# Expert gate and up weights read as one 16 KB stretch per partition, with the gathered rows turned by every fourth column

## The chip, the cores and the metric

The kernel runs on one core of a Trainium2 chip. The metric is device time in microseconds (us) of one execution. All weights and activations are float32; TensorE works on them either as float32 or, where a value has been split into a high and a low part, as rounded float32.

## The reference

The program is two transformer blocks; the change concerns the first, which has two layers (`DEPTH = 2`). In each layer 512 tokens of 1,024 values go through a modulated norm, attention and a convolution, and then through sixteen experts that each pick their own 64 tokens:

```python
def expert_choice_ffn(h, w_router, w_gate, w_up, w_down):
    cap = CAPACITY_FACTOR * S // N_EXPERTS                     # 64
    aff = jax.nn.softmax(jnp.einsum('bsd,de->bse', h, w_router), axis=-1)
    gate, idx = lax.top_k(aff.transpose(0, 2, 1), cap)
    xe = jax.vmap(lambda hb, ib: hb[ib])(h, idx)               # gathered rows
    hid = jax.nn.silu(jnp.einsum('becd,edf->becf', xe, w_gate)) * jnp.einsum('becd,edf->becf', xe, w_up)
    ye = jnp.einsum('becf,efd->becd', hid, w_down) * gate[..., None].astype(h.dtype)
    ...                                                        # scattered back and added
# in the layer: h2 = rms_norm(x, norm2_g[l]) * (1.0 + scale2) + shift2
```

`w_gate`, `w_up` and `w_down` are each 1,024 by 1,024 for each expert and layer, 4 MB in float32, so the experts of one layer need 192 MB.

## The kernel before

One pass of the loop over the layers is a block in which each engine has its own instruction stream, and all waits are semaphore waits written by hand. SyncE (SP) issues nearly all transfers, in program order, on one queue.

**The experts' weights.** Each of the three matrices of an expert is read in two halves, so an expert `e` has six chunks of 2 MB, `j` = 0, 1 (gate), 2, 3 (up), 4, 5 (down). A chunk lies as 128 partitions by 4 by 1,024 values, 16 KB in each partition. `load(e, j)` issues one. For down, partition p takes four neighbouring rows of the matrix, which lie in memory as one run of 16 KB (`(h p k)`); for gate and up it takes rows p, p + 128, p + 256, p + 384 of the half, four runs of 4 KB (`(h k p)`). There are six places in the tile `ring` and two early ones; a chunk is loaded into a place as soon as TensorE has used the chunk that stood there (`chunk_used`). Eight chunks (six of expert 0, gate of expert 1) are read before the experts begin; each of the other 88 follows a use.

**The tokens.** Experts are worked in pairs `n`. `gather(n)` picks 128 token rows out of `h_high3` and `h_low3`, which hold x / rms(x), and puts them in PSUM; ScalarE copies them to `x_rows` [128 rows, 1,024]. `turn_tokens(n)` turns them in 8 pieces of 128 columns, so that the width stands on the partitions; VectorE multiplies by `smod` (norm gain times 1 + scale2) and adds `mod` (shift2), which both hold one value for each (partition, kt), and writes `x_e`. `expert` then multiplies: for each chunk j and each k of 4, two products of 64 stationary columns with 512 moving values. The sum over the width runs over partition and k, so rows of weights and pieces of tokens have to be cut in the same way. `hidT` is already turned by every fourth column (`hid_apart`) to fit the down weights.

**The place of the small products.** In the attention part, TensorE (from line 663 on) makes tiles of values (L663), then the router's bias (`mod` times `w_r`, L684, into PSUM bank 3), then waits for VectorE's `kd` (L1211) and spreads the first head's key factors (L679). VectorE multiplies the first head's keys by them (L1217, L1218), and the scores and the softmax (L711, L1233, L993) follow. VectorE copies the router's bias out of bank 3 in the first step of the softmax loop (L1252).

Of the kernel before, what the change touches and what calls it, by code (L numbers as in the profile page):

```python
# [12 lines left out]
P = 128  # L13
D = 1024
KT = D // P
S = 512
TT = S // P
# [9 lines left out]
EXPERTS, CAP = 16, 64  # L27
# [20 lines left out]
SHIFT1, SCALE1, GATE1, SHIFT2, SCALE2, GATE2 = (m * KT for m in range(N_MOD))  # L48
# [3 lines left out]
GROUP = 32  # L52
# [235 lines left out]
def layer(nc, A, sem, M, l, ahead):  # L288

    ps, const, xT, ring, scr = M["ps"], M["const"], M["xT"], M["ring"], M["scr"]
    ident, rot = const[:, C_IDENT:C_IDENT + P], const[:, C_ROT:C_ROT + P]
# [10 lines left out]
    vec, convw, mod, smod = (M[n] for n in ("vec", "convw", "mod", "smod"))  # L303
# [41 lines left out]
    GATHER_BANKS = (0, 5)  # L345
# [15 lines left out]
    rbias = M["rbias"]  # L361
    rankm, gcol = M["krg_r"][0:EXPERTS, :], M["gcol"]
    sel_pair = M["hy_r"][0:EXPERTS, 7 * S - P:7 * S]
    x_e, sg, hid = (scr[:, 0, :], hy[:, 7 * S:8 * S]), scr[:, 1, :], scr[:, 2, :]
    x_rows = hy[:, D:2 * D]
    hidT, hid_apart = sg, hid.rearrange("p (n b) -> p b n", b=4)
    s_pair = M["scr_r"][:, 3, :].rearrange("p (t n) -> p t n", t=TT)
    h_high3 = M["one_hot_T_r"][:, 0:CHUNK].rearrange("p (t d) -> p t d", t=TT)
# [3 lines left out]
    c_spread, ada_used, ada_rows, ada_cols, mod_ready = (sem(n) for n in ("c_spread", "ada_used", "ada_rows", "ada_cols", "mod_ready"))  # L372
# [16 lines left out]
    r_bias_mm, r_bias_kept, r_scaled, xe_scaled, sel_built = (sem(n) for n in ("r_bias_mm", "r_bias_kept", "r_scaled", "xe_scaled", "sel_built"))  # L389
# [21 lines left out]
    with nc.Block() as block:  # L411
        @block.sync
        def _(sp):
            w_ada = at("w_ada").rearrange("a (k p) n -> p (a k) n", p=P)
            w = at("w_in").rearrange("a (k p) n -> p (a k) n", p=P)

            def ada_chunk(c):
                before = max(b for b in range(c) if ADA_PLACES[b] == ADA_PLACES[c])
                sp.wait_ge(ada_used, before + 1)
                sp.dma_start(ada[c], w_ada[:, :, HALF * c:HALF * (c + 1)]).then_inc(ada_in[ADA_PLACES[c]], 16)  # L420

            load_input(sp, A, M, l, w_in_in)
            ada_chunk(4)
            for piece, then in ((2, (5,)), (CT, (6,)), (3, range(7, 12))):
                if piece < CT:
                    for i in (2 * piece, 2 * piece + 1):
                        sp.dma_start(w_in[i], w[:, :, in_cols[i]:in_cols[i] + P]).then_inc(w_in_in[piece], 16)
                else:
                    sp.wait_ge(ahead["tables"], 16)
                    sp.dma_start(ring[:, CHUNK:CHUNK + KT * first].rearrange("p (k n) -> p k n", k=KT), w[:, :, 0:first]).then_inc(w_in_in[piece], 16)  # L430
                for c in then:
                    ada_chunk(c)
            sp.wait_ge(ada_used, 12)
            sp.dma_start(w_uq, at("w_uq").rearrange("a (k p) n -> p (a k) n", p=P)).then_inc(uq_in, 16)
            sp.dma_start(w_ukv, at("w_ukv").rearrange("a p n -> p (a n)")).then_inc(uq_in, 16)
            sp.dma_start(ring[:, TABLES:TABLES + 2 * S], A["rope"]).then_inc(uq_in, 16)
            sp.dma_start(w_r[:, :, 0:EXPERTS], at("w_router").rearrange("a (k p) n -> p (a k) n", p=P)).then_inc(w_r_in, 16)
            w = at("w_out").rearrange("a (k p) n -> p (a k) n", p=P)
            for k in range(0, KT, 4):
                sp.dma_start(w_out[:, k:k + 4], w[:, k:k + 4]).then_inc(w_out_in, 16)  # L440

            def load(e, j):
                name, half = ("w_gate", "w_up", "w_down")[j // 2], j % 2
                w = A[name][bass.ds(l, 1), bass.ds(e, 1)]
                if name == "w_down":
                    w = w.rearrange("a e (h p k) n -> h p (a e k) n", h=2, k=4)
                else:
                    w = w.rearrange("a e (h k p) n -> h p (a e k) n", h=2, k=4)
                place, landed, _ = expert_chunk(e, j)
                sp.dma_start(place, w[half]).then_inc(landed, 16)  # L450

            sp.wait_ge(pv_done, HEADS)
            for j in (1, 2, 3):
                load(0, j)
            sp.wait_ge(cmix, CT)
            load(1, 1)
            sp.wait_ge(wout_done, KT)
            for e, j in ((0, 0), (0, 4), (0, 5), (1, 0)):
                load(e, j)
            for n in range(6):  # L460
                sp.wait_ge(chunk_used, n + 1)
                load(1 + (n + EARLY) // 6, (n + EARLY) % 6)

            with sp.If(l < DEPTH - 1):
                load_rows(sp, A, M, (l + 1) % DEPTH, ahead)
            with sp.If(l > DEPTH - 2):
                sp.wait_ge(chunk_used, 8)
                sp.dma_start(mem_tok, A["mem_2"][0].rearrange("(t p) d -> p t d", p=P)).then_inc(mem_in, 16)
                for i, name in enumerate(("ln_mem_g_2", "ln_mem_b_2")):
                    sp.dma_start(rowsA[KT * i:KT * (i + 1), :], A[name].rearrange("(k p) -> k p", p=P)).then_inc(mem_in, 16)  # L470

            def shifted(e, j):
                sp.wait_ge(chunk_used, 6 * e + (j - 5))
                load(e, j)

            for j in range(EARLY, 6):
                shifted(2, j)
            with sp.Fori(3, EXPERTS) as e:
                for j in range(6):
                    shifted(e, j)  # L480
            with sp.If(l < DEPTH - 1):
                after, used = (l + 1) % DEPTH, 6 * EXPERTS
                for c in range(3):
                    sp.wait_ge(chunk_used, used - (5 - c))
                    load_ada(sp, A, M, after, c, ahead)
                sp.wait_ge(xe_mm, 2 * PAIRS)
                load_ada(sp, A, M, after, 3, ahead)
            with sp.If(l > DEPTH - 2):
                sp.wait_ge(st_mm, PAIRS)
                load_mixer(sp, A, M, ahead)  # L490
# [23 lines left out]
        def _(pe):  # L514
# [49 lines left out]
            for at_tile, i in enumerate(IN_ORDER):  # L564
                bank = at_tile % 6
                if at_tile == 0:
                    pe.wait_ge(w_in_ready, 2)
                    for kt in range(KT):
                        pe.wait_ge(h_low_ready, kt + 1)
                        for n in range(2):  # L570
                            pe.matmul(ps[:, n, :], w_in_high[n][:, kt, :], h_high[:, kt, :], start=(kt == 0), stop=False)
                            pe.matmul(ps[:, n, :], w_in_high[n][:, kt, :], h_low[:, kt, :], start=False, stop=False)
                            mm = pe.matmul(ps[:, n, :], w_in_low[n][:, kt, :], h_high[:, kt, :], start=False, stop=(kt == KT - 1))
# [41 lines left out]
            for i in range(10):  # L615
# [6 lines left out]
                out = ps[:, i % 6, :]  # L622
# [57 lines left out]

            pe.wait_ge(w_r_in, 16)
            pe.wait_ge(pad_zero, 1)
            for kt in range(KT):
                mm = pe.matmul(ps[:, 3, 0:GROUP], mod[:, SHIFT2 + kt:SHIFT2 + kt + 1].to_broadcast([P, P]), w_r[:, kt, :], start=(kt == 0), stop=(kt == KT - 1))  # L684
            mm.then_inc(r_bias_mm, 1)
# [117 lines left out]
            def turn_tokens(n):  # L803
                for half in range(2):
                    pe.wait_ge(xe_kept, 2 * n + (half + 1))
                    for b in range(4):
                        kt = 4 * half + b
                        mm = pe.transpose(ps[:, GATHER_BANKS[half], b * P:(b + 1) * P], x_rows[:, kt * P:(kt + 1) * P], ident)
                    mm.then_inc(xeT_mm, 1)

            def gates(n):
# [288 lines left out]
        def _(dve):  # L1100
# [129 lines left out]
            for i in range(4 * HEADS + 1):  # L1230
# [18 lines left out]
                        next(conv)  # L1249
                if i == 0:  # L1250
                    dve.wait_ge(r_bias_mm, 1)
                    dve.tensor_copy(rbias[:], ps[:, 3, 0:EXPERTS]).then_inc(r_bias_kept, 1)  # L1252
                if 7 <= i < 7 + KT:
                    kt = i - 7
                    dve.wait_ge(w_out_split, kt + 1)
# [60 lines left out]
            def build(n, ranks):  # L1316
                dve.tensor_tensor(s_pair.rearrange("p t (r s) -> p t r s", r=2), slot_row.rearrange("p (r s) -> p r s", r=2).unsqueeze(1).to_broadcast([P, TT, 2, CAP]),
                                  ranks[:, :, bass.ds(2 * n, 2)].unsqueeze(3).to_broadcast([P, TT, 2, CAP]), ALU.is_equal).then_inc(s_built, 1)
                for r in range(2):
# [3 lines left out]
            x_parts = [x.rearrange("p (b n) -> p b n", b=4) for x in x_e]  # L1323
            x_turned = [ps[:, bank, :].rearrange("p (b n) -> p b n", b=4) for bank in GATHER_BANKS]
            x_scale, x_shift = ([x[:, 4 * half:4 * half + 4].unsqueeze(2).to_broadcast([P, 4, P]) for half in range(2)]
                                for x in (smod[:, KT:2 * KT], mod[:, SHIFT2:SHIFT2 + KT]))

            def tokens(n):
                for half in range(2):
# [73 lines left out]
def memory1(nc, ctx, M):  # L1403
    M = dict(M)
    shared = dict(hy=[P, 2 * KT * S], h_tok=[P, TT * D], one_hot_T=[P, EXPERTS * S], ring=[P, 6 * TT * D])
    with ExitStack() as rounded:
        halves = dict(ring=[P, 3 * TT * D], ring2=[P, 3 * TT * D], scr=[P, 4, S], krg=[P, S])
        for name, shape in {**shared, **halves}.items():
            M[name + "_r"] = rounded.enter_context(nc.sbuf_tensor(name + "_r", shape, FR))
    for name, shape in dict(  # L1410
        **shared, scr=[P, 4, S],
        krg=[P, S], c_col=[P, KT], vec=[P, NVEC], convw=[P, TAPS * CT],
        mod=[P, N_MOD * KT], smod=[P, 2 * KT], stat=[P, 112],
        lg=[P, TT, EXPERTS], aff=[P, TT, EXPERTS], rankT=[P, TT, EXPERTS], top8=[EXPERTS, 8],
        gcol=[P, 2], rbias=[P, EXPERTS],
    ).items():
        M[name] = ctx.enter_context(nc.sbuf_tensor(name, shape, F32))
    return M
# [1537 lines left out]
```

## Time and profile before

| | |
|---|---|
| time, median of 3 runs | 2585.97 us (2582.03 to 2588.11) |
| the profiled execution | span 2585.9 us; no other time is given for it |
| TensorE busy | 2354.7 us, 91% of the span |
| VectorE, ScalarE, GpSimd busy | 43%, 35%, 10% |
| the DMA queue of SP | 637.98 MB, 64.9% of 16 engines' span |
| mean granted TensorE clock | 0.975 |

Busy shares are averages over stages that have different limits. The expert stages of the two layers lie at about 320 to 787 us and 1095 to 1557 us; they have to be read by themselves. A "releaser" in a row is what ended the idle time of an engine.

### The profile page before, as it was taken

How to read it: one execution, taken by the hardware profiler on the slowest of the kernel's cores; microseconds unless marked ns; L12 is line 12 of the kernel's file. 1: busy time of each engine (PE TensorE's matmuls, PEld its weight loads, DVE VectorE, ACT ScalarE, POOL GpSimd, SP SyncE). 2: the span in 40 equal slices, each digit the busy share in tenths (PEclk: the TensorE clock that was granted, in tenths of full speed). 3: DMA queues.
4: the chain of work that ended last, by engine and by line, in shares of the span. 5: the costliest groups of instructions: out<-in, count | busy, mean ns of one | idle time of the engine just before them, and what ended most of it. 6: DMA issues, size and time to landing. Idle time of an engine off the chain costs nothing. (4 is left out here: it accounts for less than half of the span.)

```text
span 2585.9 us, 31066 instructions
## 1 busy us (share of the span) xinstructions
PE 2354.7 (91%) x12565; PEld 1481.8 (57%) x12565; DVE 1124.8 (43%) x1686; ACT 913.2 (35%) x1228; POOL 268.8 (10%) x245
## 2 busy tenths in 40 slices
PE   6999799888886999799888888999999999989997
PEld 5735534333335835544333337887888777767776
DVE  4985312111214985412111225647521112459897
ACT  4256211111114256211111116656632234247775
POOL 0000100000000000100000005000254433300000
PEclk8999899999998989899999999999999999989999
DMA  9702499999999602499999995522223421159995
GB/s 343 286 1 93 168 381 415 415 416 417 417 413 345 220 1 96 164 399 415 415 417 417 416 411 170 169 82 82 82 76 100 134 66 59 56 184 378 365 366 212
DMA packets 252020, 650.48 MB, mean 252 GB/s; under 512 B 12144, under 2 KB 110718, under 8 KB 243454
## 3 DMA queue, kind: packets, MB, share of 16 engines
q1 hardware_dynamic: 248180, 637.98, 64.9%
q0 software_dynamic: 2592, 7.87, 0.8%
q10 hardware_dynamic: 1130, 2.99, 0.3%
q8 instruction: 83, 1.36, 0.2%
q14 instruction: 35, 0.29, 0.0%
HBM read 641.99 MB, written 8.39 MB: 252 GB/s over the span
## 5 line engine op out<-in xcount | busy, mean ns | idle before, releaser
L841 PE MATMUL ps<-ring,hy 128*64 128x512 f32 x992 | 225.1, 596 | 46.5 <-DMA ring<-in_w_up 31.8
L841 PE MATMUL ps<-ring,scr 128*64 128x512 f32 x992 | 225.1, 596 | 30.3 <-DMA ring<-in_w_up 28.1
L1347 DVE TENSOR_TENSOR scr<-scr,ps 128x512 f32<-128x512 f32 x32 | 22.0, 687 | 528.9 <-PE ps L841 528.9
L1614 POOL TENSOR_TENSOR raw_r<-raw,w_high 128x512 fp32r<-128x512 f32 (+1 forms) x160 | 189.8, 1219 | 435.0 <-ACT w_high L1882 435.0
L868 PE MATMUL ps<-ring,scr 128*64 128x512 f32 x1024 | 227.2, 596 | 3.1 <-ACT scr L1058 2.7
L1637 PE MATMUL ps<-x_high,w_high 128*128 128x512 f32 x464 | 186.4, 402 | 5.7 <-DVE y L2278 5.7
L1639 PE MATMUL ps<-x_high,raw_r 128*128 128x512 f32 x464 | 184.2, 397 | 0.0
L1638 PE MATMUL ps<-xT_r,w_high 128*128 128x512 f32 x464 | 183.1, 395 | 0.0
L2703 DVE TENSOR_TENSOR ring_r<-ring,ring_high 128x2048 fp32r<-128x2048 f32 x77 | 172.7, 2283 | 22.3 <-ACT ring_high L2626 22.3
L841 PEld LDWEIGHTS ps<-ring,hy 128*64 128x64 f32 x992 | 68.5, 137 | 198.2 <-issue 122.0
L841 PEld LDWEIGHTS ps<-ring,scr 128*64 128x64 f32 x992 | 68.2, 137 | 180.2 <-issue 122.2
L1135 DVE SCALAR_TENSOR_TENSOR one_hot_T<-h_tok,convw,one_hot_T 128x512 f32<-128x512 f32 x240 | 166.3, 745 | 1.8
L868 PEld LDWEIGHTS ps<-ring,scr 128*64 128x64 f32 x1024 | 70.5, 137 | 139.9 <-issue 129.1
L2626 ACT ACTIVATE ring_high<-ring 128x2048 fp32r<-128x2048 f32 x77 | 144.1, 1916 | 17.9 <-DMA ring<-in_w_up 16.4
L1882 ACT ACTIVATE w_high<-raw 128x2048 fp32r<-128x2048 f32 (+1 forms) x58 | 105.9, 1826 | 95.9 <-DMA raw<-in_p_b 48.9
L1067 ACT ACTIVATE hy<-ps,gcol 64x512 f32<-64x512 f32 x64 | 43.7, 682 | 255.7 <-PE ps L868 255.3
L1637 PEld LDWEIGHTS ps<-x_high,w_high 128*128 128x128 f32 x464 | 87.6, 189 | 27.6 <-DVE y L2278 6.2
L1638 PEld LDWEIGHTS ps<-xT_r,w_high 128*128 128x128 f32 x464 | 87.5, 189 | 22.8 <-issue 2.2
L1639 PEld LDWEIGHTS ps<-x_high,raw_r 128*128 128x128 f32 x464 | 87.4, 188 | 19.0
L2561 PE MATMUL ps<-ring_high,xg_high 128*128 128x512 f32 x224 | 92.7, 414 | 0.0
L1058 ACT ACTIVATE scr<-ps 128x512 f32<-128x512 f32 x32 | 19.1, 596 | 203.4 <-PE ps L853 203.4
L1049 ACT ACTIVATE hy<-ps 128x512 f32<-128x512 f32 x32 | 19.1, 598 | 194.3 <-PE ps L800 194.3
(589 smaller groups left out, 4582.2 us busy)
## 6 DMA issues: line engine op xcount, KB each, us to landing
ring<-in_w_up SPq DMA_DIRECT2D x64, 2048.0 KB, 23.8
ring<-in_w_down SPq DMA_DIRECT2D x64, 2048.0 KB, 22.3
ring<-in_w_gate SPq DMA_DIRECT2D x60, 2048.0 KB, 24.5
ring<-in_w_up SPq DMA_DIRECT2D x56, 1024.0 KB, 7.3
ring<-in_w_ada SPq DMA_DIRECT2D x22, 2048.0 KB, 13.3
ring<-in_w_down SPq DMA_DIRECT2D x28, 1024.0 KB, 7.4
raw<-in_w_in SPq DMA_DIRECT2D x24, 1024.0 KB, 5.1
raw<-in_w_in SPq DMA_DIRECT2D x20, 512.0 KB, 5.2
```

Source lines behind the costliest of these rows:

```text
L841: mm = pe.matmul(ps[CAP * half:CAP * (half + 1), 1 + j // 2, :], x_e[j % 2][:, at_x:at_x + CAP], weights[:, k, half * HALF:(half + 1) * HA ...
L868: mm = pe.matmul(ps[CAP * half:CAP * (half + 1), 4, :], hidT[:, at_f:at_f + CAP], weights[:, k, half * HALF:(half + 1) * HALF], start=(j = ...
L1067: made = act.activation(out[:, half * HALF:(half + 1) * HALF], ps[rows, 4, :], ACT.Identity, scale=gcol[rows, r:r + 1])
L1135: op = dve.scalar_tensor_tensor(acc[:, c, :], src, w, acc[:, c, :], ALU.mult, ALU.add)
L1614: part = pool.tensor_tensor(dst[:, a:a + 2], src[:, a:a + 2], high[:, a:a + 2].bitcast(F32), ALU.subtract)
L1637: pe.matmul(out, s_high, m_high, start=(n == 0), stop=False)
L1638: pe.matmul(out, s_high, m_low, start=False, stop=False)
L1639: mm = pe.matmul(out, s_low, m_high, start=False, stop=(n == len(terms) - 1))
L1882: act.activation(slot_of(w_high, n), landed_chunk(n), ACT.Copy).then_inc(w_split, 1)
L2561: pe.matmul(ps[:, n % 2, :], xh[i % 2][:, kt, :], h[:, k, :], start=(kt == 0), stop=False)
L2626: act.activation(high[q], raw[q], ACT.Copy).then_inc(w_split, 1)
L2703: dve.tensor_tensor(low[q], raw[q], high[q].bitcast(F32), ALU.subtract).then_inc(w_ready, 1)
```

## The change

Gate and up weights are read as down weights are: partition p takes rows 4p to 4p + 3 of a half. To fit, the gathered rows are turned by every fourth column of a half, and the two modulation vectors are put in the same order once in each layer: 32 small products with every fourth column of the identity (two vectors, four groups g, four k) write a [128, 16] piece into PSUM bank 3 beside the router's bias, and VectorE copies it into the new tile `xmod`, from which the expert part takes scale and shift.

```diff
+    x_apart = x_rows.rearrange("p (h n b) -> p h b n", h=2, b=4)
+    xmod = M["xmod"]
+    every_fourth = ident.rearrange("p (r k) -> p k r", k=4)
...
-                if name == "w_down":
-                    w = w.rearrange("a e (h p k) n -> h p (a e k) n", h=2, k=4)
-                else:
-                    w = w.rearrange("a e (h k p) n -> h p (a e k) n", h=2, k=4)
+                w = w.rearrange("a e (h p k) n -> h p (a e k) n", h=2, k=4)
...
             pe.wait_ge(pad_zero, 1)
+            pe.wait_ge(mod_ready, 3)
+            for n, vector in enumerate((smod[:, KT:2 * KT], mod[:, SHIFT2:SHIFT2 + KT])):
+                halves = vector.rearrange("p (h g) -> p g h", h=2)
+                for g in range(TT):
+                    out = ps[GROUP * g:GROUP * (g + 1), 3, GROUP + KT * n:GROUP + KT * (n + 1)].rearrange("p (h k) -> p k h", h=2)
+                    for k in range(4):
+                        pe.matmul(out[:, k, :], every_fourth[:, k, :], halves[:, g, :], start=True, stop=True)
...
-                        kt = 4 * half + b
-                        mm = pe.transpose(ps[:, GATHER_BANKS[half], b * P:(b + 1) * P], x_rows[:, kt * P:(kt + 1) * P], ident)
+                        mm = pe.transpose(ps[:, GATHER_BANKS[half], b * P:(b + 1) * P], x_apart[:, half, b, :], ident)
...
-                    dve.tensor_copy(rbias[:], ps[:, 3, 0:EXPERTS]).then_inc(r_bias_kept, 1)
+                    step(dve.tensor_copy(rbias[:], ps[:, 3, 0:EXPERTS]))
+                    dve.tensor_copy(xmod[:], ps[:, 3, GROUP:GROUP + 2 * KT]).then_inc(r_bias_kept, 1)
...
-                                for x in (smod[:, KT:2 * KT], mod[:, SHIFT2:SHIFT2 + KT]))
+                                for x in (xmod[:, 0:KT], xmod[:, KT:2 * KT]))
```

TensorE's stream in the attention part, before (each row is a group of products; `hy` holds `kd` in the row L679):

```order
L670 MATMUL ps<-const,hy 128x128 x4
L663 MATMUL ps<-ring,h_tok 128x512 x2
L684 MATMUL ps<-h_tok,mod 128x32 x8
L679 MATMUL ps<-hy,ones 128x512
L663 MATMUL ps<-ring,h_tok 128x512
```

And of the changed kernel, whose lines are numbered 7 higher from there on:

```order
L670 MATMUL ps<-const,hy 128x128 x4
L663 MATMUL ps<-ring,h_tok 128x512 x2
L689 MATMUL ps<-smod,const 32x2 x16
L689 MATMUL ps<-mod,const 32x2 x16
L691 MATMUL ps<-h_tok,mod 128x32 x8
L679 MATMUL ps<-hy,ones 128x512
L663 MATMUL ps<-ring,h_tok 128x512
```

Thirty-two calls of 32 by 2 stand ahead of the router's bias, and so ahead of the first head's key factors. Nothing else in TensorE's stream moves.

SP's stream where the first experts' chunks are issued, before:

```order
L450 DMA ring<-in_w_up 128x4x1024 x2
L450 ISA
L450 DMA one_hot_T<-in_w_gate 128x4x1024
L450 DMA ring<-in_w_gate 128x4x1024
L450 DMA ring<-in_w_down 128x4096 x2
```

And changed:

```order
L450 DMA ring<-in_w_up 128x4096 x2
L450 ISA
L450 DMA one_hot_T<-in_w_gate 128x4096
L450 DMA ring<-in_w_gate 128x4096
L450 DMA ring<-in_w_down 128x4096 x2
```

The order of the transfers stays; the gate and up rows now have the shape that down has, one run for each partition instead of four.

## Rows read from the trace of the kernel before

**Rows 1.** Busy time by stretch, whole expert stages and pieces of the first one.
```profile
core 0: us, PE busy (x) PEld busy (x) DVE busy (x) ACT busy (x) POOL busy (x), PEclk, DMA share, GB/s
320.40:787.00 466.60, 422.26 (x1967) 172.21 (x1971) 99.00 (x178) 60.40 (x92) 0.00 (x0) 1.00 1.01 407
336.00:436.00 100.00, 99.31 (x475) 41.48 (x476) 19.58 (x37) 14.52 (x22) 0.00 (x0) 1.00 1.00 404
436.00:536.00 100.00, 90.22 (x424) 38.80 (x422) 22.17 (x37) 11.51 (x18) 0.00 (x0) 1.00 1.02 415
636.00:736.00 100.00, 87.72 (x412) 35.97 (x410) 18.66 (x34) 12.56 (x19) 0.00 (x0) 1.00 1.02 416
```

**Rows 2.** TensorE's waits in each expert stage: total us, times, longest.
```profile
PE ps L841 <- DMA ring<-in_w_up: 29.9, 22, 1.5
PE ps L841 <- DMA ring<-in_w_gate: 7.4, 5, 1.5
...
PE ps L841 <- DMA ring<-in_w_up: 30.0, 22, 1.5
PE ps L841 <- DMA ring<-in_w_gate: 7.3, 5, 1.5
```

**Rows 3.** TensorE in time order: first wait for weights, a free-running expert, last chunk.
```profile
389.12 7.09 PE L868 MATMUL ps<-ring,scr 128*64 128x512 f32 x32
416.44 7.09 PE L868 MATMUL ps<-ring,scr 128*64 128x512 f32 x32
456.95 3.65 PE L841 MATMUL ps<-ring,scr 128*64 128x512 f32 x16 [1.44 <-DMA ring<-in_w_up]
774.67 3.65 PE L868 MATMUL ps<-ring,scr 128*64 128x512 f32 x16 [0.17 <-DMA ring<-in_w_down]
```

**Rows 4.** Packets of three stretches: 836 to 850, 1191 to 1204, 1207 to 1214 us.
```profile
DMA packets 2667, 5.42 MB, mean 387 GB/s; under 512 B 33, under 2 KB 33, under 8 KB 2664
DMA packets 1334, 5.32 MB, mean 410 GB/s; under 512 B 34, under 2 KB 34, under 8 KB 1334
DMA packets 202, 3.05 MB, mean 435 GB/s; under 512 B 16, under 2 KB 16, under 8 KB 16
```

**Rows 5.** Busy time by stretch: one kind of transfer in each.
```profile
835.00:850.00 15.00, 15.00 (x178) 12.26 (x177) 11.03 (x15) 3.05 (x5) 0.00 (x0) 1.00 1.04 387
1191.00:1204.00 13.00, 13.00 (x66) 4.56 (x64) 5.49 (x11) 2.42 (x3) 0.00 (x0) 1.00 1.03 410
1207.00:1214.00 7.00, 7.00 (x34) 3.03 (x31) 1.64 (x3) 0.00 (x0) 0.00 (x0) 1.00 1.02 435
1237.50:1244.00 6.50, 6.50 (x29) 3.46 (x30) 0.69 (x1) 0.60 (x1) 0.00 (x0) 1.00 0.99 423
```

**Rows 6.** All engines in time order around the router's bias, layer 0.
```profile
159.96 1.87 PE L684 MATMUL ps<-h_tok,mod 128*128 128x32 f32 x16
162.60 1.13 PE L679 MATMUL ps<-hy,ones 128*128 128x512 f32 x2 [0.77 <-DVE hy L1211]
165.27 1.12 PE L711 MATMUL ps<-ring 128*128 128x512 f32 x2 [0.69 <-ACT ring L986]
171.00 0.17 DVE L1252 COPY rbias<-ps 128x16 f32<-128x16 f32 x1
```

**Rows 7.** Small products: a run of 32 by 128, and L684's single durations.
```profile
213.68 1.08 PE L517 MATMUL ps<-scr,ones 128*32 128x128 f32 x32
...
L684 PE MATMUL ps<-h_tok,mod x32: 193/276/277, 160.0 to 932.0; 128*128 128x32 f32 x32
```

**Rows 8.** Groups of the turns, strided (L853) and not (L808), 400 to 750 us.
```profile
L853 PE MATMUL ps<-const,scr 128*128 128x128 f32 x48 | 7.6, 280 | 0.0
L808 PE MATMUL ps<-const,hy 128*128 128x128 f32 x48 | 6.6, 280 | 0.0
```

**Rows 9.** Busy time by stretch: the same 155 us of the two layers.
```profile
155.00:310.00 155.00, 129.51 (x626) 74.49 (x616) 86.58 (x166) 77.44 (x135) 9.85 (x8) 0.96 0.27 108
926.00:1081.00 155.00, 134.48 (x614) 75.44 (x610) 82.81 (x159) 77.29 (x134) 9.85 (x8) 0.92 0.25 98
```

More of the change, by code:

```diff
@@ L1414, in memory1 @@
         lg=[P, TT, EXPERTS], aff=[P, TT, EXPERTS], rankT=[P, TT, EXPERTS], top8=[EXPERTS, 8],
-        gcol=[P, 2], rbias=[P, EXPERTS],
+        gcol=[P, 2], rbias=[P, EXPERTS], xmod=[P, 2 * KT],
     ).items():
```

## The prediction

> **What bounds the kernel now.** I read the busy time by stretch first. In the expert stage of the first layer the DMA engines are busy for a share of 1.01 and TensorE for 422 of 467 us [rows 1]. The pieces of that stage differ: from 336 to 436 us TensorE is busy 99.31 of 100 us and the transfers run at 404 GB/s; from 436 us on TensorE has 10 to 12 us of idle time in each 100, and the transfers stand at 415 to 416 GB/s. The second view, TensorE's waits, says what ends that idle time: in each layer 37.3 us are waits for gate and up chunks (29.9 + 7.4, and 30.0 + 7.3) [rows 2]. In time order the first such wait comes at 456.95 us, and the last down chunk is still waited for at 774.67 us [rows 3]. So for the first five experts TensorE lives on the eight chunks read ahead, and then the DMA queue sets the pace. One expert that waits for nothing takes TensorE 416.44 - 389.12 = 27.3 us [rows 3] (every second one has less beside it and takes less), while its 12.58 MB at 415.5 GB/s take 30.3 us.
>
> The third view is the DMA traffic of stretches that hold one kind of transfer. From 1191 to 1204 us there are 1,300 larger packets in 5.32 MB, 4 KB each: gate and up. From 1207 to 1214 us there are 186 of 16 KB: down. From 836 to 850 us, modulation weights come in packets of 2 KB [rows 4]. With the engines always busy, the three move at 387 (2 KB), 410 (4 KB) and 435 or 423 GB/s (16 KB, two stretches) [rows 5]. A window of 7 us over packets of 16 KB is coarse, so I work out their rate from the long windows: one expert is 30.28 us at 415.5 GB/s [rows 1], its four chunks of 4 KB packets take 4 x 2.097 MB / 410 = 20.46 us, so its two down chunks take 9.82 us, 4.91 us each, or 427 GB/s. A gate or up chunk takes 5.115 us.
>
> **The change part by part.**
>
> *The transfers.* A gate or up chunk becomes what a down chunk is now, in shape, size and destination. I price it at 4.91 us: 0.205 us less. Of a layer's 64 gate and up chunks, six are read ahead while TensorE does other things (four of expert 0, two of expert 1), at no gain; 58 follow a use. If the queue never ran dry that would be 58 x 0.205 = 11.9 us per layer. It does run dry at first: the 404 GB/s of 336 to 436 us against 415.5 [rows 1] is 2.8 us in which transfers waited for TensorE to free a place. There a faster transfer only waits sooner. That stretch serves 3.3 experts, 0.82 us each, so up to 2.7 us of the gain may be lost there; as most of the idle time there lies in few gaps, I take 0.9. That leaves 11.0 us per layer (9.2 to 11.9), 22.0 us for both. It fits under the waits that it shortens, 37.3 us per layer, and an expert would still take the queue 29.5 us against 27.3 of TensorE, so the queue stays the bound. What comes behind the stage hangs on its end: the last down chunk (its wait is at 774.67 us), then the scatter and the next layer. SP's next transfers wait for the same uses and come forward with them. So I count the gain in full.
>
> The rate has two ends: with 435 GB/s a chunk takes 4.82 us and the gain is 58 x 0.295 - 0.9 = 16.2 us per layer; with 423 GB/s it takes 4.96 us and the gain is 58 x 0.157 - 0.9 = 8.2. I stay at 427, which comes from 300 us and not from 7.
>
> The Trainium skill speaks against this term: DMA: Bandwidth & Descriptors, Specifications, gives 512 B as the least transfer for line rate, by which 4 KB pieces are already at full rate and longer ones bring nothing. By that rule this trace should show equal rates; it shows 410 for 4 KB and 427 for 16 KB, and disagrees.
>
> *The added products.* 32 calls, each two instructions as everywhere in float32 (8 calls of L684 are 16 instructions [rows 6]), so 64 per layer. None of this shape is in the trace. L517 has the same 32 stationary columns and a wider moving side: 32 instructions in 1.08 us, 34 ns each [rows 7]. But its neighbours go to four different groups of columns in turn, the added ones four times in a row to the same group. L684, with 128 stationary columns, is the other end: 16 in 1.87 us, 117 ns each [rows 6]. From below 64 x 34 ns = 2.2 us, from above 7.5 us. They are nearest to L517; I take 45 ns, 2.9 us.
>
> Where they stand, that is nearly all on the path. TensorE ends L684 at 161.83 us and waits 0.77 us for `kd`, which comes at 162.54 [rows 6]; this slack hides the first 0.77 us. The rest, 2.1 us, delays the key factors (L679), behind them the fourth tile of values, ScalarE's copy of it, and the scores, which wait for that copy already now (0.69 us, at 165.27 us). Behind the scores stand the softmax of all heads, w_out and the router. Only when w_out is done does SP issue the last chunks ahead, and the experts start from the router, so nothing takes the delay back.
>
> *VectorE's copy.* One more copy of 128 by 16: 0.17 us [rows 6], between taps and the second maximum. I put 0.1 us of it on the path (0 to 0.2). The new wait for `mod_ready` was passed before, at the broadcast of the latent norms, and costs nothing.
>
> *The turns.* They read `x_rows` with a step of four. The turn of `hid` does that now (L853): 280 ns on average, as L808 without a step: 280 ns [rows 8]. Nothing. `xmod` instead of `smod` and `mod` changes no size.
>
> Sum per layer: -11.0 + 2.1 + 0.1 = -8.8 us; two layers -17.6. The profiled span is 2585.9 us, the median 2585.97 us, so both serve: 2568.3 us.
>
> **The rivals.**
>
> 1. *The added products run at the spacing of L684.* 7.5 - 0.77 + 0.1 = 6.8 us per layer: 2585.9 - 22.0 + 13.6 = 2577.5. For it: four neighbours in one group of columns. Against it: a quarter of the columns to load.
>
> 2. *The granted clock.* The same 155 us of the two layers have 0.96 and 0.92 of full speed, and TensorE is busy 129.51 and 134.48 us in them, although they do the same work [rows 9]: about 5 us hang on where the clock falls to the lower of its two levels, 1.2 GHz. The change moves and slightly alters TensorE's activity right at the start of this stretch. One such fall more or less: 2573.3 or 2563.3. Nothing in the rows says which.
>
> 3. *The transfers gain nothing.* If gate and up reads are slow for where they lie and not for their packets, the queue stays at 415.5 GB/s, and only the added work remains: 2585.9 + 4.4 = 2590.3, 0.17% slower. Against it: the three rates rise with packet size, and all three are reads of the same kind of tensor.
>
> 4. *The other side: the added products don't overlap at all.* One alone takes 276 ns (L684) [rows 7]; the 117 ns are its spacing. If each waits for the end of its neighbour, because both go to the same group and bank, 64 x 0.276 = 17.7 us stand ahead of the key factors, 17.0 per layer on the path: 2585.9 - 22.0 + 34.0 = 2597.9, slower by 0.5%. It decides from (11.0 + 0.77) / 64 = 184 ns each. Against it: L684's neighbours go to one place too, all into the same sum, and overlap.
>
> **How the numbers follow.** The likeliest case (transfers at 427 GB/s, products at 34 to 60 ns) has 0.66, rival 1 has 0.10, rival 2 has 0.07 for each sign, rival 3 has 0.06, rival 4 has 0.04. The predicted time is that of the first, 2568.3 us. Its own range, from the queue's loss at the start (9.2 to 11.9), the products (2.2 to 3.8 us) and half of the way to the two rates, is 2562 to 2574. Over all, the low side reaches to 2558 (435 GB/s gives 2557.9), the high side to 2578, past rival 1. What a measurement of this kernel can tell from no change is about 0.2%, 5 us. Faster by more than that: all but rivals 3 and 4, 0.90. Rival 3 lies within 0.2%: 0.06. Slower: 0.04.
>
> **What the profile of the changed kernel would show.** The packets of the expert stages are 16 KB for all six chunks and the rate in each 100 us is 427 GB/s; at 418 or less the first term is more than three quarters off. TensorE's waits for gate and up are about 26 us per layer. Each expert stage is about 11 us shorter. The added products take 2.2 to 3.8 us in each layer, the wait of L679 for `kd` is gone, and from their start to the start of the expert stage the time is 2.2 us longer, at the same clock. The prediction is wrong if the rate stays at 415, if the products take over 7 us, or if TensorE's waits vanish and the stage doesn't get shorter, which would mean that TensorE is the bound before I think so.

## The result, and the profile after

The changed kernel takes 2570.18 us (median of 4 runs, 2564.83 to 2573.45), the kernel before 2587.01 us beside it. The ratio of the runs is 0.9946, with a 95% interval of 0.9932 to 0.9960: 14 us, or 0.54%, faster (the two medians by themselves lie 16.8 us apart). The profiled execution has a span of 2571.7 us, 14.2 us less than before. Of all executions used below one is left out, of the kernel `products_only`, which took 6070 us.

The busy time by stretch, the same 100 us windows and the same columns as before [rows 1]:

```profile
336.00:436.00 100.00, 98.45 (x470) 41.46 (x468) 18.86 (x35) 13.93 (x21) 0.00 (x0) 1.00 0.98 410
436.00:536.00 100.00, 94.39 (x444) 40.56 (x441) 20.88 (x37) 12.10 (x19) 0.00 (x0) 1.00 1.01 428
636.00:736.00 100.00, 91.02 (x425) 37.58 (x422) 19.23 (x35) 12.56 (x19) 0.00 (x0) 1.00 1.01 429
```

The queue runs at 428 to 429 GB/s where it ran at 415 to 416, and TensorE's idle time there is smaller. The packets of a stretch that held gate and up chunks before (1191 to 1204 us) are now 16 KB (338 larger packets in 5.54 MB), and the waits of TensorE in the first and in the second expert stage are shorter and come later, the first at 467.40 us (456.95 before [rows 3]):

```profile
DMA packets 375, 5.54 MB, mean 426 GB/s; under 512 B 37, under 2 KB 37, under 8 KB 37
```
```profile
PE ps L847 <- DMA ring<-in_w_up: 20.3, 21, 1.2
PE ps L847 <- DMA ring<-in_w_gate: 5.5, 5, 1.1
...
PE ps L847 <- DMA ring<-in_w_up: 20.6, 21, 1.3
PE ps L847 <- DMA ring<-in_w_gate: 5.5, 5, 1.1
```
```profile
467.40 3.65 PE L847 MATMUL ps<-ring,hy 128*64 128x512 f32 x16 [0.58 <-DMA ring<-in_w_up]
```

TensorE around the router's bias in layer 0, in order of time (before: [rows 6]; L691 is the router's bias, L718 the first scores):

```profile
159.51 1.26 PE L689 MATMUL ps<-smod,const 128*32 128x2 f32 x29
160.78 1.24 PE L689 MATMUL ps<-mod,const 128*32 128x2 f32 x29
161.95 2.75 PE L691 MATMUL ps<-h_tok,mod 128*128 128x32 f32 x16
164.51 2.05 PE L679 MATMUL ps<-hy,ones 128*128 128x512 f32 x2
168.96 2.08 PE L718 MATMUL ps<-ring 128*128 128x512 f32 x2 [0.69 <-ACT ring L992]
```

The added products take 161.95 - 159.51 = 2.44 us, 38 ns per instruction, and L679 waits for nothing any more. But the router's bias takes 2.75 us where it took 1.87, L679 takes 2.05 us where it took 1.13, and the first scores come 3.7 us later than before: behind the products the granted clock is at the lower level in this execution. Three windows show it, one of the kernel before and two of the changed one:

```profile
163.50:180.00 16.50, 13.48 (x33) 4.32 (x31) 13.43 (x27) 7.55 (x15) 0.00 (x0) 1.00 0.00 0
```
```profile
163.50:180.00 16.50, 15.81 (x22) 5.33 (x21) 7.82 (x16) 4.43 (x8) 0.00 (x0) 0.50 0.00 0
155.00:310.00 155.00, 138.64 (x678) 78.77 (x674) 79.72 (x154) 76.87 (x133) 7.68 (x7) 0.92 0.22 89
```

Cutting both executions at three places in each layer (the start of the turns L670, the start of the first expert's first product, the end of the last down product), from the starts of those rows, gives where the 14.2 us are:

| stretch, us | before | after | difference |
|---|---|---|---|
| start to L670 of layer 0 | 157.81 | 157.26 | -0.6 |
| L670 to the experts, layer 0 | 162.63 | 170.73 | +8.1 |
| experts, layer 0 | 457.88 | 446.52 | -11.4 |
| to L670 of layer 1 | 149.89 | 150.69 | +0.8 |
| L670 to the experts, layer 1 | 167.27 | 170.76 | +3.5 |
| experts, layer 1 | 458.22 | 446.78 | -11.4 |
| second block | 1032.20 | 1028.96 | -3.2 |

So the transfers give 22.8 us, the two stretches with the added products take back 11.6 us, and the rest is spread. How much of the 11.6 us belongs to the products and how much to this one execution, a second profile of the same kernel tells (`after_again`, another execution):

```profile
161.74 1.97 PE L691 MATMUL ps<-h_tok,mod 128*128 128x32 f32 x16
166.19 1.12 PE L718 MATMUL ps<-ring 128*128 128x512 f32 x2 [0.69 <-ACT ring L992]
```
```profile
163.50:180.00 16.50, 14.35 (x36) 4.82 (x35) 12.55 (x27) 6.54 (x13) 0.00 (x0) 1.00 0.00 0
```

Here the clock is at full speed behind the same products. From L670 (at 157.05 us) to the first scores it is 9.14 us, against 7.46 us in the kernel before and 11.70 us in the first profile. So at full clock the products cost 1.7 us on the path, and the 2.6 us beside them in the first profile went with the clock.

### The profile page after: what moved, and what is told of

It is laid out like the page before. It is cut to its first block and busy times, and to the rows that moved or that the text cites. A ratio compares the mean times of both kernels' runs of the same rounds, so it can differ in the third digit from the quotient of the medians.

```text
span 2571.7 us, 31324 instructions
## 1 busy us (share of the span) xinstructions
PE 2371.3 (92%) x12693; PEld 1495.2 (58%) x12693; DVE 1126.1 (44%) x1688; ACT 912.9 (35%) x1228; POOL 268.7 (10%) x245
## 5 line engine op out<-in xcount | busy, mean ns | idle before, releaser
L847 PE MATMUL ps<-ring,hy 128*64 128x512 f32 x992 | 225.0, 595 | 37.1 <-DMA ring<-in_w_up 26.1
L847 PE MATMUL ps<-ring,scr 128*64 128x512 f32 x992 | 224.5, 594 | 16.8 <-DMA ring<-in_w_up 14.7
L2570 PE MATMUL ps<-ring_high,xg_low 128*128 128x512 f32 x224 | 87.7, 392 | 0.0
```

The costliest lines, as they stand in the source:

```text
L847: mm = pe.matmul(ps[CAP * half:CAP * (half + 1), 1 + j // 2, :], x_e[j % 2][:, at_x:at_x + CAP], weights[:, k, half * HALF:(half + 1) * HA ...
L2570: mm = pe.matmul(ps[:, n % 2, :], xl[i % 2][:, kt, :], h[:, k, :], start=False, stop=(kt == KT - 1))
```

## The experiments

All ratios are of a kernel's runs to runs of the kernel before on the same chip.

### The parts alone: `transfers_only`, `products_only`

```diff
 transfers_only: the changed kernel, and
-            pe.wait_ge(mod_ready, 3)
-            for n, vector in enumerate(...):  ... 32 products
-                    dve.tensor_copy(xmod[:], ps[:, 3, GROUP:GROUP + 2 * KT])...
-                                for x in (xmod[:, 0:KT], xmod[:, KT:2 * KT]))
+                                for x in (smod[:, KT:2 * KT], mod[:, SHIFT2:SHIFT2 + KT]))
 products_only: the kernel before, with the 32 products and the copy
```

> The changed kernel without the 32 added products and the second copy; scale and shift are taken from smod and mod in their old order, so the tokens are modulated wrongly. Theory 1 (the transfers give the gain, and the added products cost more than their own 2.4 us per layer, because the granted clock falls right behind them): both expert stages stay 11.4 us shorter than before, the stretches ahead of them are as before, so 2587.0 - 22.8 = 2564.2 us, ratio 0.9912, and the fall of the clock at 163 us of layer 0 is gone. Rival (the clock fell there by chance of its phase): the products' own 1.7 us per layer are saved, 2570.2 - 3.4 = 2566.8 us, and the clock may fall anywhere.

> The kernel before with the 32 added products and the second copy in each layer, and nothing else; what they make is not used. Theory 1: the clock falls behind them in both layers, as it does in the changed kernel, so +8.0 and +3.4 us as its trace has them: 2598.4 us, ratio 1.0044. Rival: only what they take beyond the wait that they fill, 1.8 us per layer: 2590.6 us, ratio 1.0014, with the clock at full speed behind them in layer 0.

`transfers_only`: 2562.8 us, ratio 0.9920 (0.9901 to 0.9938). Its expert stages are 447.63 and 447.60 us. The ratio doesn't decide: theory 1 gives 0.9912 and the rival 0.9922, and both lie in the interval. The stages are 10.3 and 10.6 us shorter than before, of the 11.4 that were expected. But the clock did fall in its layer 0 (its stretch from L670 is 167.04 us, as long as that of layer 1 before, and its clock from 155 to 310 us is 0.93), so a fall there needs no products. That part of theory 1 is refuted as it was put.

`products_only`: 2590.37 us, ratio 1.0028 (1.0015 to 1.0040). By the ratio it is 7.2 us more (3.9 to 10.3), between the two theories' 3.6 and 11.4, and the interval holds neither. Its expert stages are 458.06 and 458.15 us, as before. Where its clock hardly fell (layer 0), the stretch from L670 is 165.35 us, 2.7 more than in the kernel before; in layer 1 it is 170.58 us, 3.3 more.

### The products elsewhere, and more of them: `products_late`, `products_x4`, `late_x4`

```diff
 products_late: the changed kernel, the products moved behind turn_rows, ahead of the wait for the ranks
+                    out = ps[GROUP * g:GROUP * (g + 1), 7, 2 * P + KT * n:2 * P + KT * (n + 1)].rearrange("p (h k) -> p k h", h=2)
             pe.wait_ge(rank_ready, 1)
...
             step(dve.tensor_copy(rankT[:], turned))
+            step(dve.tensor_copy(xmod[:], ps[:, 7, 2 * P:2 * P + 2 * KT]))
 products_x4 (at the change's place), late_x4 (at the late place):
-            for n, vector in enumerate((...)):
+            for n, vector in 4 * tuple(enumerate((...))):
```

> The changed kernel with the 32 products put where TensorE waits 10.5 us for the ranks (L796 in the changed kernel), into bank 7, and copied there. Both theories: the products cost nothing there. Theory 1: no fall of the clock at 163 us either, so as without the products: 2564.2 us, 0.9976 of the changed kernel, ratio to before 0.9912. Rival: 2566.8 us. If the products in the new place lie on the path after all, 2 to 3 us per layer more.

> The changed kernel with the 32 products made four times over in each layer (the same values written again). They take 2.44 us once in the trace, so 7.3 us more per layer: 2570.2 + 14.6 = 2584.8 us by both theories, ratio to before 0.9992. If it is the sparse work of these products that makes the clock fall (theory 1), four times as much makes it fall earlier, partly within them, and for longer: another 2 to 5 us per layer, up to 2594 us. By the rival nothing beyond the 14.6 us.

> The changed kernel with the products in TensorE's wait for the ranks, as before, but made four times over there. Their work of 4 x 2.6 us just fills the 10.5 us of the wait. Theory 1 (it is the place that costs, not the products): no time more than with the products late once, ratio 0.9915, within 1 us per layer, and the clock at 0.974. Rival (products of this kind lower the clock wherever they stand): mean clock 0.969 as with four times in front, and 3 to 6 us more.

`products_late`: 2560.0 us, ratio 0.9915 (0.9899 to 0.9931). It has the lowest time of the kernels that leave nothing out. TensorE makes the products where it waited 10.47 us for the ranks, and still waits:

```profile
298.28 1.26 PE L792 MATMUL ps<-smod,const 128*32 128x2 f32 x29
308.63 0.60 PE L795 MATMUL ps<-const,krg_r 16*128 16x16 f32 x4 [7.84 <-DVE krg_r L1317]
```

The stretches from L670 to the experts are 162.52 and 164.11 us, the lowest of all profiles; in `late_again`, the same kernel, they are 165.64 and 167.25 us. There the ratio is 0.9911 (0.9892 to 0.9930). The ratios of both theories, 0.9912 and 0.9922, lie in both intervals; from 163.5 to 180 us the clock is at full speed in both profiles, as theory 1 had it, but that is so in `after_again` too.

> The kernel with the products late, beside the kernel before on one more chip. Ratio 0.9915 (0.990 to 0.993), mean clock 0.974, expert stages of 447 us, rank stretch of both layers 1.9 us plus the clock's share shorter than in the changed kernel.

`products_x4`: 2583.34 us, ratio 1.0000 (0.9989 to 1.0011), so 14 us more than the changed kernel's 0.9946 has, and 16 more than the 0.9937 of its second measurement; 14.6 were expected by the rival. Of the 2 to 5 us per layer that theory 1 put on top, the upper part is refuted: 2594 us would be a ratio of 1.0027, above the interval. In its trace the four rounds take 8.84 us in each layer, 6.4 more than one round's 2.44, so 12.8 of the 14 to 16 us are the rounds themselves, and little is left for the clock (part of its lower level lies over the added products there, which don't notice it, as the last section shows). `late_x4`: 2561.65 us, ratio 0.9918 (0.9898 to 0.9937), as late once. The three more rounds, 192 instructions in each layer, cost about 15 us at the one place and nothing that can be told at the other: it is the place. The clock speaks for that too: `late_x4` has a mean of 0.973, the 0.974 of theory 1 and not the rival's 0.969.

### The packets: `runs_8k`, `runs_2k`, `down_4k`

The tokens of these three are turned as in the changed kernel, so their expert outputs are other ones; the work of the engines and the bytes are the same. In `runs_8k` and `runs_2k` the place in the ring is cut in the same way as the weights.

```diff
 runs_8k, gate and up:
+                    w = w.rearrange("a e (h k p q) n -> h p (a e k) (q n)", h=2, k=2, q=2)
 runs_2k, gate and up:
+                    w = w.rearrange("a e r (c n) -> a e (r c) n", c=2).rearrange("a e (h k p) n -> h p (a e k) n", h=2, k=8)
 down_4k, down only:
+                    w = w.rearrange("a e (h k p) n -> h p (a e k) n", h=2, k=4)
```

> The changed kernel with gate and up read in two runs of 8 KB per partition (weights and tokens no longer fit together, so the output of the experts is another). Theory 1 (each packet costs a fixed 8.4 ns beside its bytes: 4 KB at 410 GB/s is 159.8 ns per engine, 16 KB at 427 is 613.9, so 0.0370 ns per byte and 8.4 ns): 8 KB take 311 ns, 421 GB/s, a chunk 4.98 us, and each expert stage is 58 x 0.07 = 4 us longer than the 446.7 of the changed kernel: 451 us; 2578 us in all. Rival (what counts is that a partition's rows lie in one piece, not the length of the packets): the 458 us of before; 2593 us.

> The changed kernel with gate and up read in eight runs of 2 KB per partition (again another output). Theory 1: 2 KB take 75.7 + 8.4 = 84.1 ns, 390 GB/s, a chunk 5.38 us, 58 x 0.47 = 27 us more per stage than 446.7: 474 us; 2625 us in all. Rival (a partition's rows in one piece or not): as with 4 KB, 458 us and 2593 us. A second rival (runs shorter than the 4 KB of before are no worse, since the engines fill a packet from several): also 458 us.

> The changed kernel with the down weights read as gate and up were before, in four runs of 4 KB per partition (another output), so the two kinds have changed places. Theory 1: 30 down chunks of a layer behind the start take 0.205 us more each, 6.2 us: stages of 453 us and 2582.5 us in all. Rival (it was gate and up, whose chunks TensorE waits for, and down chunks are never late, so their length costs nothing): stages of 447 us, 2570 us.

| kernel | gate, up / down packets | expert stages, us | expected | ratio |
|---|---|---|---|---|
| `runs_2k` | 2 / 16 KB | 474.0, 475.5 | 474 | 1.0148 (1.0133 to 1.0162) |
| before | 4 / 16 KB | 457.9, 458.2 | | 1 |
| `down_4k` | 16 / 4 KB | 453.2, 454.1 | 453 | 1.0002 (0.9990 to 1.0014) |
| `runs_8k` | 8 / 16 KB | 450.7, 450.3 | 451 | 0.9976 (0.9962 to 0.9990) |
| after | 16 / 16 KB | 446.5, 446.8 | | 0.9946 (0.9932 to 0.9960) |

The rates from 536 to 636 us in `runs_8k`, `runs_2k` and `down_4k`:

```profile
DMA packets 4728, 42.40 MB, mean 424 GB/s; under 512 B 320, under 2 KB 320, under 8 KB 320
```
```profile
DMA packets 13546, 40.05 MB, mean 400 GB/s; under 512 B 313, under 2 KB 313, under 8 KB 12643
```
```profile
DMA packets 5233, 42.28 MB, mean 423 GB/s; under 512 B 326, under 2 KB 326, under 8 KB 3428
```

One law with two numbers, 8.4 ns per packet and 0.0370 ns per byte on each engine, both from the 4 KB and 16 KB rates of the kernel before, added to the 446.7 us of the changed kernel, gives all three stages within 1.5 us. The rivals would have had 458 us for the first two and 447 for the last. Since the down chunks count as gate and up do, it is the sum of the queue's work that sets the stage, not which chunk TensorE waits for. In all these kernels a packet is one contiguous run of memory, so a price for each packet can't be told here from a price for each jump in the addresses; what is shown is that the rate rises with the length of the run.

### The clock: `after_again`, `transfers_again`

> The changed kernel as it is, beside the kernel before on one more chip, to set its time and its mean clock beside those of the kernels with the products late, alone and four times. Theory 1 (the products cost 1.9 us per layer by themselves and as much again through the clock, which is lower for longer behind them): ratio 0.9945, mean clock some 0.002 under that of before. Rival (clock by chance): ratio 0.993 and the clock of before.

> The changed kernel without the added products again (tokens modulated wrongly), for more executions of its clock. Theory 1 (the products, where the change put them, make the clock lower for longer): without them the mean clock is that of before and of the kernel with the late products, 0.974; its first six executions had 0.9722, with a spread that leaves both open. Rival: 0.972, as the kernels with the products, and the clock has nothing to do with them. Time 2561 to 2563 us, ratio 0.992 to 0.9915.

`after_again`: 2567.83 us, ratio 0.9937 (0.9921 to 0.9953). `transfers_again`: 2560.24 us, ratio 0.9916 (0.9898 to 0.9934). The ratios decide neither case (0.9945 or 0.993, 0.992 to 0.9915); the mean clocks, 0.0020 under before and 0.9738, are those of theory 1 in both. Each execution has its mean granted clock c. As the clock has two levels, full and half, 2 x (1 - c) x its time is what it spent at the lower one:

| kernels | executions | mean clock | us at the lower level |
|---|---|---|---|
| before | 54 | 0.9745 | 132 |
| 16 KB, products left out or late | 30 | 0.9734 | 136 |
| products where the change put them | 38 | 0.9719 | 145 |
| the same, four times over | 12 | 0.9686 | 162 |

(The second row is `transfers_only`, `transfers_again`, `products_late`, `late_again`, `late_x4`, with 0.9722, 0.9738, 0.9743, 0.9732, 0.9733; the third is `products_only`, `after_again` and the three with other packets, 0.9712 to 0.9728. The four executions beside the result have 0.9708, 150 us, and are in no row.) The first six executions of `transfers_only` looked like the third row, the next six don't. With the products in front, the lower level lasts some 9 us longer in an execution than without them (standard error 2 us), with four times as many 26 us. So the clock is not a matter of chance alone, and yet the fall is not theirs either: the kernel before has one at that place in layer 1 but not in layer 0.

The profiles say the same of the time. This is the stretch from L670 to the experts in all thirteen, in us:

| kernels | layer 0 | mean | layer 1 | mean |
|---|---|---|---|---|
| before, `transfers_only`, `transfers_again`, `products_late`, `late_again`, `late_x4` | 162.6, 167.0, 162.8, 162.5, 165.6, 165.8 | 164.4 | 167.3, 167.4, 164.2, 164.1, 167.3, 167.6 | 166.3 |
| after, `after_again`, `products_only`, `runs_8k`, `runs_2k`, `down_4k` | 170.7, 165.9, 165.4, 169.0, 167.1, 167.6 | 167.6 | 170.8, 170.8, 170.6, 170.8, 170.8, 167.6 | 170.2 |
| `products_x4` | 175.4 | | 177.9 | |

One kernel differs from itself by up to 5 us in a layer (after and `after_again`), so no pair of profiles can price the products. The means can: 3.2 and 3.9 us, 7.1 for both layers, of which the products take 2 x 1.7 at full clock.

## Why the prediction was right

The time was forecast as 2568.3 us and is 2570.18 us, and 2567.83 us in a second measurement. Point by point:

- **What bounds the expert stages.** The queue, after the first experts: right (the first wait for weights came at 456.95 us, now at 467.40 us). All eight profiles with all chunks at 16 KB (five kernels) have stages of 446.4 to 447.8 us, whatever else was done.
- **The rate of 427 GB/s and a chunk of 4.91 us.** 428 to 429 GB/s measured. It was worked out from what down transfers did, and gate and up transfers then did the same.
- **11.0 us per layer, with 0.9 us lost at the start.** 11.4 us in the profiled pair; the mean over sixteen stages at 16 KB is 447.0 us against 458.1 us for four with gate and up at 4 KB, 11.1 us. The 336 to 436 us window runs at 410 GB/s, where it ran at 404, and not at 428: the loss at the start is there. From these rates it is about 1.2 us (an estimate: 1.5 of the 2.7 us that this window had to give came), against 0.9.
- **TensorE's waits of about 26 us per layer.** 25.8 and 26.1 us.
- **The added products.** 2.9 us forecast, 2.44 us measured; the wait of 0.77 us was filled, and the remainder, 1.7 us where 2.1 were forecast, reached the first scores (`after_again`, at full clock). In the layer of `products_only` in which the clock hardly fell, products, copy and the little clock cost 2.7 us together, against 2.2 forecast for the first two.
- **The turns.** Nothing, as forecast: the stages of `transfers_only` and `transfers_again`, which have the strided turns, are as short as the others.
- **What was off: the clock.** The sum has 4.4 us for the added work of both layers and nothing for the clock behind it. `products_only` measures 7.2 us (3.9 to 10.3), putting the products late gains 0.0028 of the ratio on average, 7.4 us, and the means of the profiles give 7.1. The 4.4 lies just inside the first of these intervals, but all three stand on the same side of it. Rival 2 had named the place and 5 us, but as a fall that comes more or comes less by chance. The profiled execution is such a case: 8.1 us more in layer 0, where `after_again` has 3.3. Behind that chance the runs show a bias: the lower level lasts some 9 us longer with the products there. From the two layers of before, 0.96 and 0.92 over 155 us are 12.4 us more at the lower level for 4.6 us of time, 0.37 us each; over the 54 executions of before, the time rises by 0.32 us with each us at the lower level. So 9 us are about 3 us, and with 2 x 1.7 us of products and 0.2 of copies it makes 6.6 to 6.9. That this share goes through the clock is worked out and fits; no run held the clock and moved the products.
- **The second block** ended 3.2 us shorter in the profiled execution. In the other kernels it is 1026.0 to 1033.8 us, with no order in it: scatter. In the profiled pair it was luck: with the 0.6 us at the start it made up for about half of what the clock took, and without the two the span would have been 2575.5 us, outside the forecast's own range of 2562 to 2574. The medians, of four and six executions, don't hang on it.

Rival 1 (spacing of L684) is refuted by 38 ns, rival 3 by the rates, rival 4 by the same 38 ns. The forecast of 45 ns rested on the nearest row (L517, 34 ns), as none of their own shape was there; it could have come out otherwise.

The gain that the change left on the table is the place of its products. Moved into a wait that nothing else fills, they cost nothing, and the kernel has 0.9915 and 0.9911 in place of 0.9946 and 0.9937.

## What to carry to other kernels

When one queue sets a stage's pace, sort its packets by size and look at the rate of each size apart: the trace of before held both ends of this change, since a third of the weights was already read in 16 KB runs. A matter of layout (which row goes to which partition) can often be paid for once, in a permutation of small operands. Such small work belongs where its engine waits for another anyway, and not ahead of a chain of short steps: at the first place 32 calls in each of two layers cost about 7 us, at the other nothing that can be told. And where the granted clock of a stretch differs from execution to execution, one profile of each kernel doesn't price a change in it.

## What was not expected of the hardware

- The length of a read's contiguous runs is still to be seen above 8 KB. With gate and up in runs of 2, 4, 8 and 16 KB and down always in 16 KB, the queue moves 400, 415, 424 and 428 GB/s from 536 to 636 us, with bytes, destination and queue the same. Alone, 4 KB runs move at 410 [rows 5].
- Products of 32 stationary columns and 2 moving values, some 33 ns apart in a long row of them, don't notice the clock. In `products_x4`, 26 of them take 1.06 us at 161 us and at 167 us, while the granted clock (1.00, then 0.50) has fallen between:

```profile
161.01 1.06 PE L689 MATMUL ps<-mod,const 128*32 128x2 f32 x26
...
166.34 1.06 PE L689 MATMUL ps<-smod,const 128*32 128x2 f32 x26
```
```profile
161.01:164.21 3.20, 3.20 (x103) 3.20 (x100) 1.18 (x4) 0.00 (x0) 0.00 (x0) 1.00 0.02 5
165.50:168.40 2.90, 2.90 (x91) 2.90 (x89) 0.00 (x0) 0.00 (x0) 0.00 (x0) 0.50 0.02 6
```

  So the granted clock doesn't set their pace, and what they cost beyond their own time comes from what stands behind them: the router's bias took 1.87 us before, 2.75 behind one round and 3.62 behind four, and L679 takes 2.05 in place of 1.13 us.
